# Moving the first activation buffer and the weight parts by 32 bytes within a 512-byte line

## The reference

```python
u = rms_norm(x, norm_mix_g) @ w_in                          # 2048 -> 5648
x = x + concat([ssd(u), rwkv7(u)]) @ w_out                  # 2048 -> 2048
q, k, v = h @ wq, m @ wk, m @ wv                            # each 2048 -> 2048
x = x + softmax_attention(q, k, v) @ wo
x = x + square(relu(h @ ffn_w1)) @ ffn_w2                   # 2048 -> 8192 -> 2048
proj = h @ w_in_2 + b_in_2                                  # 2048 -> 5888
merged = sigmoid(ga) * (attn @ w_branch_attn) + sigmoid(gs) * (ssm @ w_branch_ssm)
x = x + merged @ w_out_2
val, gate = split(h @ w_up_2)                               # 2048 -> 2 x 5632
x = x + (val * gelu(conv(gate))) @ w_down_2                 # 5632 -> 2048
```

## Time and profile before

| | |
|---|---|
| median of 3 runs | 2883.28 us |
| span of the profiled execution | 2882.9 us |
| TensorE busy | 2802.8 us, 24650 matmuls |
| VectorE busy | 1823.4 us |
| ScalarE busy | 1245.7 us |
| GpSimd busy | 396.0 us |
| mean granted clock of TensorE | 0.990 of full speed |

### The profile page before, as it was taken

How to read it: one execution, slowest core, us unless ns; L and a number is a source line. 1 busy time by engine, 2 the same in 40 slices (tenths; PEclk the granted TensorE clock), 3 DMA queues, 4 the chain that set the end, 5 groups by cost and what they waited for, 6 DMA issues and landing times.

```text
span 2882.9 us, 61146 instructions
## 1 busy us (share of the span) xinstructions
PE 2802.8 (97%) x24650; PEld 2752.2 (95%) x24650; DVE 1823.4 (63%) x2175; ACT 1245.7 (43%) x1511; POOL 396.0 (14%) x549
## 2 busy tenths in 40 slices
PE   8999699999999999999999999999999999999998
PEld 8999687999989999999999999998999999999998
DVE  6678747775435655655555668697667655665664
ACT  5355223544334543444434545434454443443444
POOL 0000230110002139300461210000110000010011
PEclk9999899999999999999999999999999999999999
DMA  6654002566635566666667565554555665556564
GB/s 235 195 192 147 16 31 88 191 189 204 190 102 164 190 197 190 219 213 189 197 194 236 191 195 163 193 196 157 193 192 189 197 192 193 193 188 199 184 198 149
DMA packets 138418, 514.10 MB, mean 178 GB/s; under 512 B 15360, under 2 KB 15616, under 8 KB 136960
## 3 DMA queue, kind: packets, MB, share of 16 engines
q1 hardware_dynamic: 138240, 511.58, 54.9%
HBM read 503.12 MB, written 8.40 MB: 177 GB/s over the span
## 4 chain that ended last, share of the span: by engine, by line
PE 64%; DVE 4%; issue 1%; ACT 1%; DVEq 0%; ACTq 0%
PE acc L670 21%; PE acc L671 21%; PE acc L672 21%; DVE lo L473 1%; PE work L2170 0%; ACT hi L379 0%; DVE s_xr L2514 0%; PE acc L2203 0%; DVE tb L543 0%; DVE sq L2523 0%; DVE ua L2514 0%; DVE ub L2514 0%; DVE s_xr L2505 0%; DVE sq L2503 0%; DVE ta L2522 0%
## 5 line engine op out<-in xcount | busy, mean ns | idle before, releaser
L670 PE MATMUL acc<-a,hi 128*128 128x256 f32 x5504 | 1527.0, 277 | 16.3 <-DVE lo L473 14.5
L671 PE MATMUL acc<-a,hi 128*128 128x256 f32 x5504 | 1521.5, 276 | 0.0
L672 PE MATMUL acc<-a,lo 128*128 128x256 f32 x5504 | 1521.4, 276 | 0.0
L473 DVE TENSOR_TENSOR lo<-qx,hi 128x1024 fp32r<-128x1024 f32 x704 | 896.4, 1290 | 674.6 <-ACT hi L379 672.9
L670 PEld LDWEIGHTS acc<-a,hi 128*128 128x128 f32 x5504 | 1035.3, 188 | 20.5 <-issue 14.8
L671 PEld LDWEIGHTS acc<-a,hi 128*128 128x128 f32 x5504 | 1035.3, 188 | 0.8 <-issue 0.5
L672 PEld LDWEIGHTS acc<-a,lo 128*128 128x128 f32 x5504 | 1035.3, 188 | 0.0
L379 ACT ACTIVATE hi<-qx 128x1024 fp32r<-128x1024 f32 x704 | 733.9, 1057 | 646.4 <-PE acc L672 629.0
L620 POOL TENSOR_TENSOR a<-th,a 128x512 f32 (+1 forms) x64 | 84.9, 1327 | 1381.2 <-ACT a L424 1381.1
L473 DVE TENSOR_TENSOR lo_x<-next_raw,hi_x 128x1024 fp32r<-128x1024 f32 x128 | 162.2, 1281 | 115.0 <-ACT hi_x L379 115.0
L670 PE MATMUL acc<-a,hi_in 128*128 128x256 f32 x768 | 215.4, 280 | 9.8 <-DVE lo_in L473 9.8
(11 more groups left out here) (503 smaller groups left out, 2779.2 us busy)
## 6 DMA issues: line engine op xcount, KB each, us to landing
qx<-in_ffn SPq DMA_DIRECT2D x256, 512.0 KB, 4.2
raw_in<-in_w_in SPq DMA_DIRECT2D x96, 512.0 KB, 4.3
qx<-in_w_in SPq DMA_DIRECT2D x92, 512.0 KB, 3.7
qx<-in_up_gate SPq DMA_DIRECT2D x88, 512.0 KB, 4.2
qx<-in_up_val SPq DMA_DIRECT2D x88, 512.0 KB, 4.3
qx<-in_down SPq DMA_DIRECT2D x88, 512.0 KB, 4.2
next_raw<-in_wq SPq DMA_DIRECT2D x32, 512.0 KB, 4.3
next_raw<-in_wk SPq DMA_DIRECT2D x32, 512.0 KB, 4.3
```

Source lines behind the costliest of these rows:

```text
L473: eng.tensor_tensor(self.lo[:, slot, :], self.raw[:, slot, :], self.hi[:, slot, :].bitcast(F32), ALU.subtract).then_inc(self.s_lo, 1)
L670: eng.matmul(out, self.hi[:, slot, cols], a[:, 0, :], start=opens, stop=False)
L671: eng.matmul(out, self.hi[:, slot, cols], a[:, 1, :], start=False, stop=False)
L672: ins = eng.matmul(out, self.lo[:, slot, cols], a[:, 0, :], start=False, stop=closes)
```

## The change

`a0` starts at offset 192 in the line of 512 bytes, `hi` at 256 and `lo` at 384. They stood at 160, 224 and 352. `raw`, `a1`, `a2`, `ah` and all tiles that are allocated after `stage_room` outside the rings keep their addresses, and so do `ta`, `tb`, `th` and `tq` in the rings. The tiles between `a0` and `stage_room` move by 32 bytes with `a0`.

```diff
 LINE = 512
 ACT_AT = 160
-PART_AT = ACT_AT + 64
+A0_AT = 192
+PART_AT = A0_AT + 64
...
         at = BASE + KT * T * 4
-        room = sb("a0_room", [P, (ACT_AT - at) % LINE // 4])
+        room = sb("a0_room", [P, (A0_AT - at) % LINE // 4])
...
-        at += (ACT_AT - at) % LINE + KT * T * 8 + 4 * dram["consts"].shape[1] + -(-PARAMS.n // 8) * 32 + 6 * T * 4 + 32 + KT * 4
+        at += (A0_AT - at) % LINE + KT * T * 8 + 4 * dram["consts"].shape[1] + -(-PARAMS.n // 8) * 32 + 6 * T * 4 + 32 + KT * 4
         room = sb("stage_room", [P, (ACT_AT - at) % LINE // 4])
...
         room = sb("low_room", [P, 128 // 4])
         self.lo = sb("lo", [P, RING, CK * UNIT], F32R)
-        room = sb("end_room", [P, (LINE - 128) // 4])
+        room = sb("end_room", [P, (LINE - 128 - A0_AT + ACT_AT) // 4])
```

## The result

The changed kernel takes 2919.5 us (median of 4 runs, 2918.6 to 2919.8) against 2883.35 us for the kernel before (now 4 runs): a ratio of 1.0124, 95% interval 1.011 to 1.0138. It is 36 us slower, where no change was forecast. The profiled execution spans 2917.6 us, 34.7 more than the 2882.9 of before.

What follows compares the result with a forecast made beforehand. TensorE, busy 2802.8 of 2882.9 us, was taken as the bound: a count of matmuls times their period. All five terms were taken as 0, giving 2883 us, with a range of 2850 to 2924.

Steps and rivals of the forecast that it cites:

- The reading of the period from counts: TensorE's matmuls in `unit`: period from instructions touched in uniform stretches, 113.3 ns, v projection 117.7; it counts 22272 times.
- Item 1: Split into high and low parts on ScalarE and VectorE: 0, at most 2.4 us either way.
- Item 2: The 2378 matmuls outside `unit`, some reading moved tiles: 0, upper bound 4.8 us.
- Item 3: Phases on `a1`, `a2`, `ah`, 7872 matmuls, weights 32 bytes on, moving operand unchanged: 0.
- The bound of item 3: Most that phases on `a1`, `a2`, `ah` could lose: 3 ns × 7872 = 23.6 us, from L667's 279 against 276 ns.
- Item 4: Phases on `a0`, 13632 matmuls, both operands moving together, distances kept: 0, at most 64 us of gain.
- Item 5: v projection, 768 matmuls, distances kept: 0, at best 3.4 us saved, at worst 4.2 us lost.
- the second one: Slower: operand distance decides, in phases not moving along (`a1`, `a2`, `ah`); 2907 us, or 2891 with a third; chance 0.09.
- The first one: Slower: the moving operand's start decides, 2.75 ns a matmul in all `a0` phases, 37.5 us, 2921 us; chance 0.17.
- The third: Faster: starts at multiples of 64 shed part of 6.7 ns in `a0` phases; up to 64 us, 2819; chance 0.24.
- looks like a floor: `a0` phases: 113.3 ns a matmul, met with different rings, buffers and weight offsets, taken as a reason to forecast 0.

Runs made afterwards that it cites:

- 512 series: TensorE alone on zeros: ten triples each, all 256 pairs of distances, weights stationary and turned round, in two drawn orders; 272 cycles a matmul in both orders for six pairs.
- the pair 64, 64: Kernel before with the low weight parts at the high ones' offset, 224, so both distances from the activations are 64: 2923.8 us, median of six runs.

## Why the prediction was wrong, point by point

- The reading of the period from counts, and that everything hangs on it: right. The change moved 34.2 us of TensorE's busy time and nothing else.
- Item 1 (split): right. 1289 and 1056 ns, the waits for weight parts within 0.6 us of the earlier trace rows.
- Item 2 (small float32 products): right. The first mixers, from the end of z_in to the start of w_out, take 150.6 us before and 150.8 after.
- **Item 3 is the step that failed.** It said that weights at 224 and 352 cost the same, that 256 lies between, and that the term is therefore 0. It treated the cost as a smooth function of the offset, to be read between two points, and for each matmul alone. The runs show neither. The pair acts on the whole triple, the fast rhythm exists for a few pairs only, and 96, 224 isn't one. The argument wasn't even one of two points: 224 and 352 are seen only together, as one pair in one rhythm, and two of the three loads, not one, come from 224. That all three matmuls are equally long follows from their running in one rhythm, whatever the offsets: in the changed kernel they are nearly equal too, at 280, 281 and 279 ns. The term is 7872 × 4.45 ns = 35.0 us in place of 0.
- The bound of item 3 was too low as well, 23.6 us. I had taken the 3 ns by which L667 is longer as the price of the distance 320, once more a single matmul's. The period of the v projection, 4.4 ns over the others, stood in the earlier trace rows and gives 34.6 us.
- Item 4 (`a0` phases): right, 113.3 ns after as before, and for the stated reason, the distances kept. The kernel with `a0` alone moved shows that it was the reason.
- Item 5 (v): right, 682 in 80 us in both.
- The rivals: the second one had the right thing, the distances, and the right phases, with a chance of 0.09 and at most 2907 us; by its right price it would have been 2918. Its sign came, fewer matmuls in ffn2 alone, 682 where it had 690. But it too took the price from how near a distance comes to 320, and nearness isn't it: the pairs 320, 192 and 320, 320 are fast with weights stationary. The first one, 2921 us, hit the time by luck, for a wrong reason: it laid the loss in the `a0` phases, which lost nothing, and the kernel with all tiles 32 bytes on, moving starts at 192, took 2884.4 us. That 2919.5 us lies under the 2924 up to which the range went is the same luck, since the range went so far for the first rival's sake. The third, a gain from starts at multiples of 64, fell with the same kernel.
- 113.3 ns "looks like a floor": it was the lowest value in every trace and scan, but it isn't where matmuls end up by themselves.
- The rule of the Trainium skill, page "TensorE: Matmul & The Clock Gate" (Step-by-step: what each phase is for), by which loading the next weights takes nothing from the running matmul: this case's runs don't bear out what the prediction drew from it for fp32r, that the distance of the two operands is nothing. With TensorE alone, triples at start 160 ran at 113.3 ns with the pair 64, 192 and at 117.8 with 96, 224. Whether it is read bandwidth that is lost, no row shows. The prediction also named the wrong rivals beside this rule: a start that counts by itself is the mechanism of the first and the third, and the second is the distance.

What stays open: why fast pairs are found only among distances that leave 64 modulo 128 and not with all of these, what makes one pair run in one rhythm here and in another there, and what the rhythms are inside TensorE. No row shows its reads.

## What to carry to other kernels

Where TensorE is the bound, read the period of its matmuls from counts in every phase, and compare phases of the same shape: a difference (here v, 117.8 against 113.3 ns) can be a sign that addresses matter, and its price is that of the period and not of one instruction. When an operand is moved in memory, ask which of the others moves with it, for every phase that pairs them, and don't interpolate between addresses: scan them, in the pattern of the real loop and in more than one order.

## What the runs showed of the hardware that was not expected

- Triples of fp32r matmuls, 128x128 by 256 columns, run at 272 cycles a matmul (113.3 ns) or at some 277 to 299, by the distances of the two operands modulo 512. The absolute start had no part in it for the three pairs that were run at all 16 starts, and TensorE alone gave the two values of the whole kernel, 113.3 and 117.8 ns.
- One unfit operand slows the matmuls beside it: with the high part moved alone, the untouched low part's matmul takes 280 ns in place of 276; with the low part moved alone, the untouched high part's two take 281.
- The addresses alone don't fix the rhythm: 69 of 512 series differed by over 2 cycles between two runs in different orders, and the pair 64, 64 makes a kernel that takes 2906 to 2952 us from run to run.
